# Second kind of layer, mixer: the values stationary and the normalised, turned weights moving, two heads in the two column halves of the array

## What is computed

```python
def hybrid_mixer_2(h, ...):
    q_nsa, kv_nsa, g_nsa, qkv_sb, g_merge = split(h @ w_in)
    # 8 query heads of 64, 2 key-value heads (4 query heads share one), rope on q and k
    s = q @ k_cmp * hd ** -0.5           # 31 compressed positions
    o_cmp = (softmax(masked(s)) * mask) @ v_cmp
    o_slc = softmax(causal(q @ k_slc * hd ** -0.5)) @ v_slc   # at 512 tokens every block is selected
    o_win = softmax(causal(q @ k_win * hd ** -0.5)) @ v_win   # window 512: all earlier tokens
    g = sigmoid(g_nsa)
    o_nsa = g[..., 0:1] * o_cmp + g[..., 1:2] * o_slc + g[..., 2:3] * o_win
    o_sb = stick_breaking(q_sb, k_sb) @ v_sb                  # 8 heads of 64, weights need no division
    y = g_a * (o_nsa @ w_proj_nsa) + g_b * (o_sb @ w_proj_sb)
    return y @ w_out
```

## Time and profile before

| what | us |
|---|---|
| median of 3 runs (lowest to highest) | 3223.53 (3220.07 to 3224.11) |
| the profiled execution's own time | 3210.66 |
| its span, first to last instruction | 3208.9 |
| TensorE matmul busy in it | 3077.1 |
| VectorE busy | 1633.2 |
| ScalarE busy | 1235.1 |
| GpSimd busy | 1362.5 |

### The profile page before, as it was taken

The page is one execution under the profiler, slowest core; times in us unless marked ns, Lnnn a source line. Parts: engine busy times, 40 slices in busy tenths (PEclk is TensorE's granted clock), DMA queues, the critical chain, the costliest instruction groups (busy, mean ns, idle before and its releaser), DMA issues.

```text
span 3208.9 us, 39940 instructions
## 1 busy us (share of the span) xinstructions
PE 3077.1 (96%) x14974; PEld 2491.1 (78%) x14974; DVE 1633.2 (51%) x2738; ACT 1235.1 (38%) x2437; POOL 1362.5 (42%) x1167
## 2 busy tenths in 40 slices
PE   6998899999999999999999999999999999999998
PEld 5676778887766778887878787888887777778886
DVE  7787656623686553214344646554244355565521
ACT  3445332233345432233353434343335434343332
POOL 2340255545431254445442545444454234444443
PEclk9999799999999999999999999999999999999999
DMA  5422346632421123222321122323232211222222
GB/s 216 127 79 93 125 164 243 238 104 79 128 73 33 40 95 98 95 93 89 121 80 41 46 79 79 99 95 101 94 115 89 66 40 53 92 79 99 98 91 74
DMA packets 92976, 316.54 MB, mean 99 GB/s; under 512 B 12016, under 2 KB 12656, under 8 KB 92656
## 3 DMA queue, kind: packets, MB, share of 16 engines
q1 hardware_dynamic: 92784, 313.99, 29.3%
HBM read 301.36 MB, written 2.10 MB: 95 GB/s over the span
## 4 chain that ended last, share of the span: by engine, by line
PE 89%; DVE 6%; issue 2%; ACT 1%; DMA 1%; POOL 0%; SPq 0%; DVEq 0%; ACTq 0%; POOLq 0%
PE bank L199 24%; PE bank L201 23%; PE bank L200 23%; PE bank L1841 3%; PE bank L1799 2%; PE bank L1820 2%; PE bank L493 1%; PE bank L918 1%; PE bank L1080 1%; PE bank L936 1%; PE bank L1904 1%; PE bank L1905 1%; PE bank L938 1%; DMA mod_raw<-in_wmod 1%; PE bank L937 1%
## 5 line engine op out<-in xcount | busy, mean ns | idle before, releaser
L182 POOL TENSOR_TENSOR wl<-raw,wh 128x512 fp32r<-128x512 f32 (+1 forms) x952 | 1241.4, 1308 | 1677.0 <-ACT wh L171 1676.0
L171 ACT ACTIVATE wh<-raw 128x512 fp32r<-128x512 f32 (+1 forms) x952 | 587.6, 623 | 1415.2 <-PE bank L201 1319.2
L199 PE MATMUL bank<-hh,wh 128*128 128x512 f32 x2496 | 1003.6, 402 | 38.0 <-DVE hl L552 24.2
L201 PE MATMUL bank<-hh,wl 128*128 128x512 f32 x2496 | 981.9, 393 | 0.0
L200 PE MATMUL bank<-hl,wh 128*128 128x512 f32 x2496 | 981.2, 393 | 0.0
L199 PEld LDWEIGHTS bank<-hh,wh 128*128 128x128 f32 x2496 | 474.9, 190 | 165.2 <-DVE hl L552 31.0
L201 PEld LDWEIGHTS bank<-hh,wl 128*128 128x128 f32 x2496 | 473.9, 190 | 101.9
L200 PEld LDWEIGHTS bank<-hl,wh 128*128 128x128 f32 x2496 | 475.2, 190 | 95.4 <-issue 0.5
L201 PE MATMUL bank<-hidh,wl 128*128 128x512 f32 x704 | 273.9, 389 | 0.0
L199 PE MATMUL bank<-hidh,wh 128*128 128x512 f32 x704 | 273.9, 389 | 0.0
L200 PE MATMUL bank<-hidl,wh 128*128 128x512 f32 x704 | 273.9, 389 | 0.0
(11 more groups left out here) (389 smaller groups left out, 3965.1 us busy)
## 6 DMA issues: line engine op xcount, KB each, us to landing
raw<-in_w SPq DMA_DIRECT2D x444, 512.0 KB, 3.4
mod_raw2a<-in_wmod SPq DMA_DIRECT2D x28, 512.0 KB, 4.5
mod_raw2b<-in_wmod SPq DMA_DIRECT2D x28, 512.0 KB, 4.9
mod_raw<-in_wmod SPq DMA_DIRECT2D x24, 512.0 KB, 3.6
raw<-in_w SPq DMA_DIRECT2D x32, 384.0 KB, 3.0
first_mods<-in_wmod SPq DMA_DIRECT2D x16, 512.0 KB, 13.7
tmp<-rawb SPq DMA_DIRECT2D x72, 64.0 KB, 2.4
turn<-sine SPq DMA_DIRECT2D x56, 64.0 KB, 2.0
```

What stands on the lines that cost most here:

```text
L171: act.activation(self.m.wh[:, t % 2, w_], self.m.raw[:, t % RING, w_], ACT.Copy)\
L182: pool.tensor_tensor(self.m.wl[:, t % 2, w_], self.m.raw[:, t % RING, w_], self.m.wh[:, t % 2, w_].bitcast(F32), ALU.subtract)\
L199: pe.matmul(out, wh, xh, start=start, stop=False)
L201: return pe.matmul(out, wl, xh, start=False, stop=stop)
```

## The change

Four things change together in `second_mixer`.

1. In `values` the operands trade places: the values (128 keys x 64 features) are stationary, the turned weights (128 keys x 128 tokens) move. The output is feature by token: head h writes partitions 64*(h%2) to 64*(h%2)+63 of chunk h//2 of the bank, so that a pair's heads stand in the two column halves of the array; the two heads alternate within a key block. So that a pair has both halves, `soft_head` pairs head p with head (p^1)+4.
2. Sums over tokens' rows can no longer be divided after the product, so the weights are divided and gated ahead of the turn: VectorE's new `normalise(k)`, in slot k+1 between `maxima(k+1)` and `copies(k-1)`, does a reciprocal and a product on 128 x 2 and one `tensor_scalar` per head in place on the weights. `turn(k)` waits for it. `cmp_weights` gains one product, and its signal comes after four small instructions more.
3. Selected and window branch now add up in the bank (steps ordered by pair, then branch; the first branch starts the sum, the second ends it): 12 groups instead of 16, and `finish` is a copy, or for cmp one addition.
4. `turn_feature` is gone with its 32 transposes a mixer; `split_feature` reads `o_nsa` and `o_sb` from SBUF instead of the bank.

Both TensorE's `values` and the copies after them now wait for both heads of a pair. The diff, cut to its core:

```diff
@@ -1629,7 +1629,7 @@
-        steps = [("soft", tb, kind, p) for tb in range(NT) for kind in range(2) for p in range(4)]
+        steps = [("soft", tb, kind, p) for tb in range(NT) for p in range(4) for kind in range(2)]
         steps += [("cmp", tb, 0, 0) for tb in range(NT)]
@@ -1698,15 +1695,15 @@
         def soft_head(one, p):
-            h = p + 4 * one
-            return slice(64 * one, 64 * one + 64), p, h
+            c = p ^ one
+            return slice(64 * one, 64 * one + 64), c, c + 4 * one
         def sb_head(one, p):
             return slice(64 * one, 64 * one + 64), p, 2 * p + one
         def head_col(k, one):
             _, tb, kind, p = steps[k]
-            return 16 * tb + 8 * kind + (p + 4 * one)
+            return 16 * tb + 8 * kind + soft_head(one, p)[2]
@@ -1812,7 +1809,7 @@
                     if kind == "soft":
-                        pe.wait_ge(weights, i + 1)
+                        pe.wait_ge(normed, i + 1)
                     else:
@@ -1820,6 +1817,9 @@
+            def feature_of(bank, h):
+                return bank[HD * (h % 2):HD * (h % 2) + HD, (h // 2) * P:(h // 2 + 1) * P]
@@ -1829,34 +1829,28 @@
                     pe.wait_ge(bank_free[2 + one], turn_use[k, one])
-                    if kind == "cmp":
-                        continue
-                    _, _, h = (soft_head if kind == "soft" else sb_head)(one, p)
-                    for kb in range(tb + 1):
+                if kind == "cmp":
+                    for h in range(HEADS):
+                        v0 = HD * (h // 4)
+                        ins = pe.matmul(feature_of(bank, h), vct[0:NCMP, v0:v0 + HD],
+                                        ptc[tb % 2][0:NCMP, h // 4, (h % 4) * P:(h % 4 + 1) * P],
+                                        start=True, stop=True)
+                    ins.then_inc(pv, 1)
+                    return
+                for kb in range(tb + 1):
+                    for one in range(2):
+                        _, _, h = (soft_head if kind == "soft" else sb_head)(one, p)
+                        first, last = kb == 0, kb == tb
                         if kind == "sb":
                             v_ = sv2[:, kb, h * HD:(h + 1) * HD]
                         else:
-                            v0 = P * one_ + 64 * (h // 4)
+                            v0 = P * one_ + HD * one
                             v_ = vsw[:, kb, v0:v0 + HD]
-                        ins = pe.matmul(bank[:, h * HD:(h + 1) * HD], m.tmp[:, one, kb * P:(kb + 1) * P], v_,
-                                        start=(kb == 0), stop=(kb == tb))
-                    ins.then_inc(pv, 1)
-                if kind == "cmp":
-                    for h in range(HEADS):
-                        ins = pe.matmul(bank[:, h * HD:(h + 1) * HD],
-                                        ptc[tb % 2][0:NCMP, h // 4, (h % 4) * P:(h % 4 + 1) * P],
-                                        vct[0:NCMP, 64 * (h // 4):64 * (h // 4) + 64], start=True, stop=True)
-                    ins.then_inc(pv, 1)
-
-            def turn_feature(f):
-                of, tb = f
-                bank = feat_use[f]
-                pe.wait_ge(group_done, (3 * NT if of else 2 * NT) + tb + 1)
-                claim(bank)
-                src = (o_nsa, o_sb)[of]
-                for c in range(4):
-                    ins = pe.transpose(ps[bank][:, c * P:(c + 1) * P], src[:, tb, c * P:(c + 1) * P], ident)
-                ins.then_inc(feat_turned, 1)
+                            first, last = first and one_ == 0, last and one_ == 1
+                        ins = pe.matmul(feature_of(bank, h), v_, m.tmp[:, one, kb * P:(kb + 1) * P],
+                                        start=first, stop=last)
+                        if kb == tb:
+                            ins.then_inc(pv, 1)
@@ -2082,10 +2072,23 @@
                 step(dve.tensor_reduce(csum[:, tb, :], c, AX_X, ALU.add))
-                dve.tensor_tensor(c, c, cm.unsqueeze(1).to_broadcast([P, HEADS, NCMP]), ALU.mult)\
-                   .then_inc(cweights, 1)
+                step(dve.tensor_tensor(c, c, cm.unsqueeze(1).to_broadcast([P, HEADS, NCMP]), ALU.mult))
                 step(dve.reciprocal(csum[:, tb, :], csum[:, tb, :]))
                 step(dve.tensor_tensor(csum[:, tb, :], csum[:, tb, :], gts[:, tb, :, 0], ALU.mult))
+                dve.tensor_tensor(c, c, csum[:, tb, :].unsqueeze(2).to_broadcast([P, HEADS, NCMP]), ALU.mult)\
+                   .then_inc(cweights, 1)
+
+            def normalise(k):
+                kind, tb, one_, p = steps[k]
+                at, apart = head_col(k, 0), head_col(k, 1) - head_col(k, 0)
+                factor = col8[:, 0:2]
+                dve.wait_ge(weights, first_item[k] + 2)
+                step(dve.reciprocal(factor, den[:, at:at + apart + 1:apart]))
+                step(dve.tensor_tensor(factor, factor, gts[:, tb, p:p + apart + 1:apart, 1 + one_], ALU.mult))
+                for one in range(2):
+                    pr_ = prs[(first_item[k] + one) % 6][:, 0:(tb + 1) * P]
+                    dve.tensor_scalar(pr_, pr_, col8[:, one:one + 1], None, ALU.mult).then_inc(normed, 1)
+                dve.wait_ge(normed, first_item[k] + 2)
@@ -2117,7 +2120,7 @@
                 if k:
-                    dve.wait_ge(pv, first_item[k - 1] + 1)
+                    dve.wait_ge(pv, first_item[k - 1] + 2)
                 dve.tensor_copy(m.tmp[:, 0, 0:w_], ps[2][:, 0:w_]).then_inc(bank_free[2], 1)
@@ -2125,36 +2128,19 @@
                 dve.wait_ge(pv, upto(k + 1))
-                if kind == "sb":
-                    step(dve.tensor_copy(o_sb[:, tb, :], bank[:]))
-                    dve.sem_inc(bank_free[6 + g % 2], 1)
-                    dve.sem_inc(group_done, 1)
-                    return
-                if kind == "soft":
-                    at = 16 * tb + 8 * one_
-                    step(dve.reciprocal(col8, den[:, at:at + 8]))
-                    step(dve.tensor_tensor(col8, col8, gts[:, tb, :, 1 + one_], ALU.mult))
-                    factor = col8
+                if kind == "cmp":
+                    step(dve.tensor_tensor(o_nsa[:, tb, :], o_nsa[:, tb, :], bank[:], ALU.add))
                 else:
-                    factor = csum[:, tb, :]
-                first = kind == "soft" and one_ == 0
-                dst = o_nsa[:, tb, :] if first else m.acc[:]
-                step(dve.tensor_tensor(heads_of(dst), heads_of(bank[:]), by_head(factor), ALU.mult))
+                    step(dve.tensor_copy((o_sb if kind == "sb" else o_nsa)[:, tb, :], bank[:]))
                 dve.sem_inc(bank_free[6 + g % 2], 1)
-                if not first:
-                    step(dve.tensor_tensor(o_nsa[:, tb, :], o_nsa[:, tb, :], m.acc[:], ALU.add))
-                dve.sem_inc(group_done, 1)
-
-            def evict_feature(f):
+
+            def split_feature(f):
                 of, tb = f
-                bank = feat_use[f]
                 hi, lo = ((fnh, fnl), (fsh, fsl))[of]
-                dve.wait_ge(feat_turned, 1 + tb + NT * of)
-                src = ps[bank][:].rearrange("p (c t) -> p c t", c=4)
+                src = (o_nsa, o_sb)[of][:, tb, :].rearrange("p (c t) -> p c t", c=4)
                 ts_ = slice(tb * P, (tb + 1) * P)
                 step(dve.tensor_copy(hi[:, :, ts_], src))
                 step(dve.tensor_tensor(lo[:, :, ts_], src, hi[:, :, ts_].bitcast(F32), ALU.subtract))
-                dve.sem_inc(bank_free[bank], 1)
                 dve.sem_inc(feat_ready, 1)
@@ -2179,6 +2165,8 @@
                     maxima(n)
+                if 0 <= n - 1 < len(steps) and steps[n - 1][0] == "soft":
+                    normalise(n - 1)
                 if 0 <= n - TURN_LAG < len(steps):
@@ -2192,7 +2180,7 @@
                 for f in features(n):
-                    evict_feature(f)
+                    split_feature(f)
```

More of the change, by code:

```diff
@@ L1604, in build @@
         "cmp_ready", "gates", "score", "weights", "turned", "pv", "cshift", "cexp", "cweights",
-        "keeps", "keeps_masked", "betas_masked", "suffixes", "products", "group_done", "feat_turned", "feat_ready",
+        "keeps", "keeps_masked", "betas_masked", "suffixes", "products", "normed", "feat_ready",
         "order")
@@ L1612, in second_mixer @@
          cmp_ready, gates, score, weights, turned, pv, cshift, cexp, cweights,
-         keeps, keeps_masked, betas_masked, suffixes, products, group_done, feat_turned, feat_ready,
+         keeps, keeps_masked, betas_masked, suffixes, products, normed, feat_ready,
          order) = sems[8:]
@@ L1647, in second_mixer @@
             items += 1 if kind == "cmp" else 2
-            g = 2 * tb + one if kind == "soft" else 2 * NT + tb if kind == "cmp" else 3 * NT + tb
+            g = tb if kind == "soft" else NT + tb if kind == "cmp" else 2 * NT + tb
             group_of.append(g)
             last_of[g] = k
-        first_of = {g: group_of.index(g) for g in range(4 * NT)}
```

(14 more changed lines are left out.)

## The result

| | before | changed |
|---|---|---|
| median, us (lowest to highest, runs) | 3222.30 (3220.07 to 3224.11, 4) | 3179.02 (3170.89 to 3180.06, 4) |
| profiled execution: own time / span | 3210.66 / 3208.9 | 3170.89 / 3169.2 |
| mean granted clock in it | 0.972 | 0.970 |

The ratio is 0.9862, 95% interval 0.9846 to 0.9879. The change saves 43 us by the medians and 40 by the profiled executions, where the sum said 71: inside the range, but at the place of the rivals, "the column mode drains" (3186) and "loads don't hide in a column tile" (3179), not at the forecast of 3152.5.

A forecast was written before the change was run, and what follows sets the result against it. TensorE was taken to bound the kernel; savings of 54.3, 7.2 and 13.5 us less 4 gave 71, so 3223.5 - 71 = 3152.5 us. The forecast's own range was 3140 to 3166, the stated saving range 3138 to 3209.

The forecast's parts named there:

- the sum: Whole kernel: savings of 54.3, 7.2 and 13.5 us less 4 for VectorE's added work give 71 us.
- the column mode drains: Rival: passages into and out of column halves in 96 steps cost 34 us, leaving 37 saved, 3186 us; chance 0.15.
- loads don't hide in a column tile: Rival: each value record takes 0.055 + 0.107 = 0.162 us, saving 44, 3179 us; chance 0.05.
- What bounds the kernel: TensorE, at 96% of the span, bounds the whole kernel, so work it need not do comes off the time.
- Values: Value products: a pair's heads overlap fully in column halves, saving 54.3 us in soft and sb steps, 7.2 in compressed ones.
- halves taking turns: Rival: the array reads one moving stream at a time, so values gain only 2 us besides 13.5; 3208 us, chance 0.16.
- each half is a mode of its own: Rival: alternating heads drains at all 544 products, 84 us, giving 3292; chance 0.06 together with another slower case.
- Entering and leaving the halves: Passages between the full array and column halves around the values: taken as 0, with 34 us as the other bound.
- The row change: Going to or from row halves, as at scores: 0.15 us in and 0.2 out, 34 us if applied to 96 steps.
- Feature transposes: Removing 64 transposes saves 7.0 us, and TensorE's waits for their bank 6.5 more, 13.5 us in all.
- VectorE: Normalising weights ahead of the turn costs 4 us in both mixers, in the compress stretch; bounds no loss and 26 us.

The follow-up runs named there:

- heads_in_turn: The changed kernel with a pair's second head begun only after the first has done all key blocks: 3192.18 us, ratio 0.9888 to the kernel before.
- one_half: The changed kernel using only the first column half for all heads, one after the other, branches not added: 3236.30 us, ratio 1.0054 to the kernel before.
- compress_fp32: The kernel before with compress tiles in plain fp32, one product in place of three passes: 3236.0 us in one run.
- the run alone: The kernel before without the feature transposes, the splits reading unturned outputs: 3205.41 us, ratio 0.9957.

## Why the prediction came out as it did

**What bounds the kernel**: held. TensorE kept 96% of the span.

**Values**: held, as far as the pair's overlap goes. I took full overlap from the row halves; sixteen records take 1.09 us against 1.90, and with one half alone the attention takes 56 us more. The rival of halves taking turns falls, and so does "each half is a mode of its own": alternating is the cheaper of the two orders tried, as heads_in_turn shows. Loads do hide: in one_half eight value records span 1.09 us, the distances of their starts being 0.160 and six times 0.109, on average 0.116, not 0.162. So the rival with that price, 3179, has the measured time and not the mechanism. (Its sum charges 2 for VectorE where the forecast charges 4; with the 4 it is 3181. The sum of the halves in turn leaves VectorE out; with the 4 it is 3212.)

**Entering and leaving the halves**: this is the step that failed. "Both are changes of the array's tile; the second changes columns only, as this change does, so I take 0." The row that I took as nearest, from the 128 columns of the values to the 32 of the compress tile, costs nothing because of its format, as compress_fp32 shows: that tile is fp32r, and in plain fp32 the same tile of the same shape comes 0.20 us after the last matmul instead of 0.084. The row change, which I kept as the other bound with 0.35 us a step, was the right neighbour: the passages cost 0.24, or 23 us in 96 steps. The other 8 us of the missing 31 are the count of records: "the weight load of 128 columns sets this pace" holds for six of eight, while the first record of a step cost 0.058 and the last 0.084, so 0.08 a step was never there to save. The rival "the column mode drains" came to 3186; the kernel runs at 3179. The rule of the Trainium skill that I set against the change (TensorEngine Tiling, Key Properties: a switch of the tiling mode drains TensorE) holds for this change, by the gaps of 0.17 us in the loads; I let one row overrule it that did not show the case. The other rule of the Trainium skill that I named (TensorE: Matmul & The Clock Gate, Part 3: loads hide only where the row group differs) does not hold here, by the 0.116.

**Feature transposes**: 13.5 forecast, 8 to 19 by the run alone, and 23.69 to 17.96 us in the stretch of the first mixer.

**VectorE**: 4 forecast; some 2 by the rows, 2.4 and 4.8 by times too coarse to tell. The size was about right and the working was not. I had VectorE at 19.7 to 24.3 us in the compress stretch, and it is 22.84, but the small product on 128 x 2 waits for GpSimd too, which I had priced at 0.17 us throughout (shortest, median and longest of 64, in ns):

```profile
L2087 DVE TENSOR_TENSOR sm<-sm x64: 161/178/1257, 1579.3 to 2556.9; 128x2 f32<-128x2 f32 x64
```

All 31 that took over 0.2 us end within 0.03 us of the end of the GpSimd subtraction into which they fell. The product reads two operands from SBUF, and the earlier trace rows show a long case (0.869) of a larger one; the one-operand reciprocal of the same shape beside it never takes more than 0.165. And one instruction behind the copy that I hadn't named, a small turn at L1866 that comes once a mixer, has the largest of TensorE's waits for these copies:

```profile
PE bank L1866 <- DVE tmp L2124: 2.5, 2, 1.3
```

It is 2.5 us in both mixers together, 1.7 without the division; in the kernel before the same turn waits 0.14 us a mixer.

**The sum**, corrected by the runs: 54.3 + 7.2 + 13.5 - 4 - 23 - 8 = 40, measured 40 by the profiled executions and 43 by the medians (39 to 50 by the interval). The second mixers' stretches give 36 + 3.5 = 39.5 at equal clock, which is what the terms can be held against; the drops of the clock in the kernel before, some 4 us on average, were no term of mine and could make it 43. The stated range held the time because it reached to the rivals' places; the forecast's own range, 3140 to 3166, did not. The compressed steps owed nothing at their ends, since they had paid already.

## What to carry to other kernels

Before a product is moved into halves of the array, count the passages between whole array, row halves and column halves in a slot, at some 0.1 us each beyond the pace and 0.05 for an uncovered first load, and set them against what the halves save there: here 0.23 us for each key block of 128 against 0.32 lost, so a step with one block loses and those with two to four win. Then order the steps so that kinds which cost a passage anyway stand side by side: scores, values, turn saved another 17.6 us (3160.09, 0.9796 of the time before). And when a row of the trace is taken as the neighbour of an operation that it does not show, compare the format of the operands too, not the shape alone.

## What the runs showed of the hardware

- A stationary of 32 columns in fp32r followed the whole array in step; the same in fp32 came 0.20 us after the last matmul. The matmul rows' types read `f32` for both, so the program has to be read for it.
- The gap is the same for 64 and 32 columns, at column 0 or at 0 and 64: 0.17 us without a load on the way in.
- A turn behind the scores and values behind the scores both start their loads 0.33 us after the end of the scores' loads: coming out of row halves costs no more when the next step is in column halves.
- Two column halves ran at once in fp32 with both heads moving 128 columns, when the heads alternate; issued one after the other they overlapped in part (1.58 us against 1.09 and 1.9), the second head's first record starting beside the one four places ahead of it in the program, before the first head was through (0.494 against 0.815 us).
- A VectorE `tensor_tensor` with two SBUF operands of 128 x 2 that fell into a GpSimd subtraction ended with it, up to 1.257 us after its start; a reciprocal of the same shape took 0.158 to 0.165 throughout.
- Left open: why the gap is as long as it is, and whether three fp32r products in place of one in fp32 would escape it at 64 columns; that was not tried.
